# Inverting the delta-rule's triangular matrix: six doubling levels of 128 columns, or blocks of 4 by Horner steps, levels on 32 stacked columns and the last level applied to the right-hand sides

## The reference

```python
def rwkv7_scan(r, w, kk, kka, k, v, s0):
    def step(S, inp):
        r_t, w_t, kk_t, kka_t, k_t, v_t = inp
        sa = jnp.einsum('bzhvk,bzhk->bzhv', S, -kk_t)
        S = S * w_t[..., None, :] + sa[..., None] * kka_t[..., None, :] + v_t[..., None] * k_t[..., None, :]
        return S, jnp.einsum('bzhvk,bzhk->bzhv', S, r_t)
    ...
```

## Time and profile before

| | |
|---|---|
| median of 3 runs | 3470.89 us (3470.37 to 3471.7) |
| the profiled execution | 3465.07 us, its span 3463.3 us |
| mean granted clock of PE | 0.978 of full speed |
| busy, share of span | PE 95%, DVE 57%, ACT 31%, POOL 15% |
| HBM traffic | 93 GB/s |

### The profile page before, as it was taken

One profiled execution on the slowest core, in us unless ns is written; L12 is line 12 of the kernel. 1 busy time (PEld: TensorE's weight loads), 2 busy tenths in 40 slices (PEclk: granted clock), 3 DMA queues, 4 the chain that ended last, 5 costly groups with the idle time before them and its releaser, 6 DMA issues.

```text
span 3463.3 us, 52254 instructions
## 1 busy us (share of the span) xinstructions
PE 3283.2 (95%) x21464; PEld 3011.0 (87%) x21464; DVE 1978.7 (57%) x2613; ACT 1083.7 (31%) x1588; POOL 525.1 (15%) x537
## 2 busy tenths in 40 slices
PE   6999999999699989999999999999988999999998
PEld 6999878978598979998789998799767988899986
DVE  5677564565555766775657774625566566522235
ACT  2211352244322252112531113523442223511134
POOL 2000110003234430001100001100213434200010
PEclk8999999999799999999999999999988999999999
DMA  5334343210000043443434434421000002222135
GB/s 203 122 145 149 135 142 134 88 36 3 26 1 10 7 160 112 155 145 120 138 132 146 152 127 144 158 82 44 24 28 1 1 10 75 92 74 81 63 110 164
DMA packets 62899, 323.81 MB, mean 93 GB/s; under 512 B 8784, under 2 KB 12688, under 8 KB 43408
## 3 DMA queue, kind: packets, MB, share of 16 engines
q1 hardware_dynamic: 62736, 321.52, 26.4%
HBM read 318.18 MB, written 3.31 MB: 93 GB/s over the span
## 4 chain that ended last, share of the span: by engine, by line
PE 81%; DVE 10%; DMA 3%; ACT 3%; issue 2%; POOL 1%; SPq 0%; DVEq 0%; ACTq 0%; POOLq 0%
PE PS L2004 42%; PE PS L2087 14%; PE PS L1331 7%; DMA wo<-in_wo 3%; PE PS L2015 3%; PE PS L648 2%; PE PS L670 2%; DVE wo_lo L2391 1%; ACT wo_hi L2192 1%; DVE macc L1845 1%; PE PS L595 1%; PE PS L658 1%; PE PS L1324 1%; PE PS L1282 1%; DVE LK L1683 1%
## 5 line engine op out<-in xcount | busy, mean ns | idle before, releaser
L2004 PE MATMUL PS<-h_hi,wi_hi 128*128 128x384 f32 (+1 forms) x3360 | 799.9, 310 | 21.7 <-issue 13.5
L2004 PE MATMUL PS<-h_lo,wi_hi 128*128 128x384 f32 (+1 forms) x3360 | 797.7, 309 | 0.0
L2004 PE MATMUL PS<-h_hi,wi_lo 128*128 128x384 f32 (+1 forms) x3360 | 797.7, 309 | 0.0
L2004 PEld LDWEIGHTS PS<-h_hi,wi_hi 128*128 128x128 f32 x3360 | 526.7, 188 | 25.2 <-issue 16.1
L2004 PEld LDWEIGHTS PS<-h_lo,wi_hi 128*128 128x128 f32 x3360 | 526.7, 188 | 0.6
L2004 PEld LDWEIGHTS PS<-h_hi,wi_lo 128*128 128x128 f32 x3360 | 526.5, 188 | 0.6
L2087 PE MATMUL PS<-wo_hi,a_hi 128*128 128x512 f32 x968 | 393.3, 406 | 20.3 <-DVE wo_lo L2391 13.3
L2391 DVE TENSOR_TENSOR wo_lo<-wo,wo_hi 128x1024 fp32r<-128x1024 f32 x208 | 256.1, 1231 | 265.0 <-ACT wo_hi L2192 264.0
L2087 PE MATMUL PS<-wo_hi,a_lo 128*128 128x512 f32 x968 | 378.5, 391 | 0.0
L2087 PE MATMUL PS<-wo_lo,a_hi 128*128 128x512 f32 x968 | 378.4, 391 | 0.0
L1845 DVE SCALAR_TENSOR_TENSOR macc<-wm,csil,macc 128x512 f32<-128x512 f32 x476 | 366.3, 769 | 16.9
(11 more groups left out here) (302 smaller groups left out, 4627.4 us busy)
## 6 DMA issues: line engine op xcount, KB each, us to landing
wi<-in_wi SPq DMA_DIRECT2D x88, 1024.0 KB, 5.0
wo<-in_wo SPq DMA_DIRECT2D x176, 512.0 KB, 3.5
wm<-in_wm SPq DMA_DIRECT2D x36, 2048.0 KB, 7.9
wi<-in_win SPq DMA_DIRECT2D x24, 1024.0 KB, 5.0
wo<-in_wout SPq DMA_DIRECT2D x32, 512.0 KB, 3.5
x<-in_x SPq DMA_DIRECT2D x1, 2048.0 KB, 26.4
wq<-in_wq SPq DMA_DIRECT2D x2, 1024.0 KB, 4.7
out_y_sample<-x SPq DMA_DIRECT2D x4, 512.0 KB, 5.7
```

The costliest lines, as they stand in the source:

```text
L2004: mm = pe.matmul(PSF[0:cols, at:at + GW[g]], st, h[g][:, k, :], start=(k == 0 and q == 0), stop=(k == KD - 1 and q == 2))
```

## The change

The inverse is found another way, per chunk:

1. **Blocks of 4 by Horner.** `LM` is now LB masked to blocks of 4 (levels 0 and 1 together, written by DVE straight from PSUM, `fours`). Three rounds X = I + LM^T X give the inverse of these blocks, since the cube is the highest power that is not zero.
2. **Stacked operands.** As long as blocks are at most 32, the 32 columns of all four diagonal blocks are stacked: `Xc` is 128 x (4 heads x 32), the identity `stack32`. Its transpose, block-diagonal, is kept in `XT`: DVE transposes each 32x32 block in place (`diagonal`, four instructions per direction and level). Levels 2, 3 and 4: t1 = near^T Xc on PE, where `near` is one mask for these levels; DVE multiplies with the packed mask of the level into T1; dx = XT^T T1 on PE, added to Xc on DVE.
3. **Level 5** goes from 32 to 64: t1 and dx on 32 columns, T1 copied by ACT, the result transposed by DVE into the off-diagonal blocks of XT.
4. **The last level is applied and not formed:** XT (two 64-blocks) is applied to R; the near half of the result times the off-diagonal block of LB (64x64 tiles of PE, both directions side by side) gives Zs; the diagonal block applied to Zs is added to the far half of X by DVE.

LK's products go to banks 0 to 3 in place of 4 to 7. POOL writes two masks per direction and chunk in place of seven. The preps stand at other places between the levels. The phase's start gains three table reductions on DVE, two memsets of XT and four additions of masks on POOL. SP's weight load waits for the second tile set (`gh_mm`) in place of the last `dxt_mm`.

```diff
@@ rwkv_tensor, inner and solve @@
                     if which:
-                        until(pe, l, f"lb{d}", c + 1)
+                        for one in ("alpha_tok", "kappa_tok", "beta_tok", "v_tok", "bv"):
+                            until(pe, l, one, c + 1)
...
+                for k in range(3):
...
+                        group(4 + 2 * d, QUAD, lambda h: LM[d][:, h, :], lambda h: Xc[d][:, h, :] if k else stack32)\
+                            .then_inc(S[f"b_mm{d}"].sem, 1)
...
+                    lk_values(c)
+                    if c + 1 < NT:
+                        prep(c + 1, 0)
+                for lv in range(2, 6):
+                    for d in range(2):
+                        until(pe, l, f"lm{d}", 2 * c + (1 if lv < 5 else 2))
+                        until(pe, l, f"x{d}", 6 * c + lv + 1)
+                        group(4 + 2 * d, QUAD, lambda h: (near if lv < 5 else LM)[d][:, h, :],
+                              lambda h: Xc[d][:, h, :]).then_inc(S[f"t1_mm{d}"].sem, 1)
+                    for d in range(2):
+                        until(pe, l, f"lb{d}", c + 1)
+                        until(pe, l, f"t1{d}", 6 * c + lv - 1)
+                        until(pe, l, f"xt{d}", 5 * c + lv - 1)
+                        group(5 + 2 * d, QUAD, lambda h: XT[d][:, h, :], lambda h: T1[d][:, h, :])\
+                            .then_inc(S[f"dx_mm{d}"].sem, 1)
+                    if c + 1 < NT and lv in (3, 5):
+                        prep(c + 1, (3, 5).index(lv) + 1)
...
-                for lv in range(1, 7):
...
+                for d in range(2):
+                    until(pe, l, f"t1{d}", 6 * c + 5)
+                for h in range(NH):
+                    for d, (a, b) in enumerate(halves):
+                        mm = pe.matmul(PS[b, 4 + 2 * d, h * P:(h + 1) * P], LB[d][a, h, 0, b], X[d][a, h, :],
+                                       start=True, stop=True)
...
+                for d in range(2):
+                    until(pe, l, f"t1{d}", 6 * c + 6)
+                for h in range(NH):
+                    for d, (a, b) in enumerate(halves):
+                        mm = pe.matmul(PS[b, 5 + 2 * d, h * P:(h + 1) * P], XT[d][b, h, b], Zs[d][b, h, :],
+                                       start=True, stop=True)
...
@@ rwkv_vector @@
+            def diagonal(d, k):
+
+                for q in range(4):
+                    at = slice(q * QUAD, (q + 1) * QUAD)
+                    m = v_.transpose(XT[d][at, :, at], Xc[d][at, :, :])
+                m.then_inc(S[f"xt{d}"].sem, 1)
+
+            def level_out(c, d, lv):
...
+                v_.tensor_tensor(xc, xc, PS[:, 5 + 2 * d, 0:P], ALU.add).then_inc(S[f"x{d}"].sem, 1)
+                mm_(f"x{d}", 6 * c + lv + 2)
+                diagonal(d, lv)
...
+                for lv in range(2, 5):
+                    for d in range(2):
+                        mm_(f"t1_mm{d}", 5 * c + lv - 1)
+                        v_.tensor_tensor(T1[d][:], PS[:, 4 + 2 * d, 0:P].rearrange("p (h t) -> p h t", h=NH),
+                                         packed[:, d, lv - 2, :].unsqueeze(1).broadcast_to([P, NH, QUAD]), ALU.mult)\
+                            .then_inc(S[f"t1{d}"].sem, 1)
+                    for d in range(2):
+                        level_out(c, d, lv)
+                    if c + 1 < NT and lv in (2, 4):
+                        prep(c + 1, (2, 4).index(lv) + 1)
+                    if c == NL and lv > 2:
+                        beside(lv - 2)
...
+                if c + 1 < NT:
+                    prep(c + 1, 3)
                 if c == NL:
...
+                    beside(3)
+                    beside(4)
+                    beside(5)
+                for d in range(2):
+                    mm_(f"gh_mm{d}", c + 1)
+                    mm_(f"t1{d}", 6 * c + 6)
+                    b = slice(64, P) if d == 0 else slice(0, 64)
+                    half_ = X[d][b, :, :].rearrange("p h t -> p (h t)")
+                    v_.tensor_tensor(half_, half_, PS[b, 5 + 2 * d, :], ALU.add).then_inc(S[f"gh{d}"].sem, 1)
...
@@ rwkv_gpsimd, sync @@
             for c in range(NT):
-                for lv in range(7):
+                for lv in range(2):
...
-                        until(sp, l, f"dxt_mm{d}", 30)
+                        until(sp, l, f"gh_mm{d}", 5)
```

More of the change, by code:

```diff
@@ new lines, in solve @@
+                if c + 1 < NT:
+                    prep(c + 1, 2)
+                if c == NL:
+                    beside(3)
+                for d in range(2):
+                    until(a_, l, f"dx_mm{d}", 5 * c + 5)
+                    a_.activation(X[d][:].rearrange("p h t -> p (h t)"), PS[:, 5 + 2 * d, :], ACT.Copy)\
+                        .then_inc(S[f"t1{d}"].sem, 1)
+                if c == NL:
+                    beside(4)
+                for d in range(2):
+                    until(a_, l, f"t1_mm{d}", 5 * c + 5)
+                    b = slice(64, P) if d == 0 else slice(0, 64)
+                    a_.activation(Zs[d][b, :, :].rearrange("p h t -> p (h t)"), PS[b, 4 + 2 * d, :], ACT.Copy)\
+                        .then_inc(S[f"t1{d}"].sem, 1)
@@ L1593, in solve @@
+                if c == NL:
+                    beside(5)
+                    beside(6)
                 for d in range(2):
@@ L1717, in solve @@
+                if c < NL:
+                    for d in range(2):
+                        for q in range(2):
+                            a, b = (2 * q, 2 * q + 1) if d == 0 else (2 * q + 1, 2 * q)
+                            v_.memset(XT[d][a * QUAD:(a + 1) * QUAD, :, b * QUAD:(b + 1) * QUAD], 0.0)
+                if c == NL:
+                    beside(6)
                 for d in range(2):
@@ L1730, in solve, with beside @@
                     m.then_inc(S[f"n_out{d}"].sem, 1)
-            for part in range(4):
+            def beside(lv):
+                if lv >= 3:
+                    rwkv_gate(v_, l, lv - 3)
+                if 2 <= lv <= 5:
+                    gn_squares(v_, l, NT + lv - 2)
+                if lv <= NL:
+                    rwkv_centre(v_, l, lv - 1)
+            prep(0, 0)
+            mm_("four", 1)
+            for d in range(2):
+                v_.reduce_sum(packed[:, d, :, :], lvl[:, 1 - d, 2:5, :].rearrange("p l (j c) -> p l c j", c=QUAD), AX)
+            v_.reduce_sum(stack32, ident[:].rearrange("p (j c) -> p c j", c=QUAD), AX).then_inc(S["packed"].sem, 1)
+            for part in range(1, 4):
                 prep(0, part)
@@ L1807, in prep_kappa @@
                 po.tensor_tensor(kd[:], kd[:], Pinv[:], ALU.mult).then_inc(S["kappa"].sem, 1)
+            until(po, l, "rs_mm", 5)
+            for d in range(2):
+                po.memset(XT[d][:], 0.0)
+            po.tensor_tensor(lvl[:, :, 1, :], lvl[:, :, 1, :], lvl[:, :, 0, :], ALU.add).then_inc(S["four"].sem, 1)
             prep(0)
             prep_kappa(0)
+            until(po, l, "packed", 1)
+            for k, done in ((3, "near_a"), (2, "near_b"), (1, "near_c")):
+                po.tensor_tensor(lvl[:, :, 4, :], lvl[:, :, 4, :], lvl[:, :, k, :], ALU.add).then_inc(S[done].sem, 1)
+                until(po, l, done, 1)
             for c in range(NT):
-                for lv in range(7):
+                for lv in range(2):
                     for d in range(2):
```

228 lines of the change are left out of this document (136 added, 92 removed).

## The result

| | before | changed |
|---|---|---|
| median | 3470.6 us (3467.2 to 3471.7, 4 runs) | 3568.9 us (3566.2 to 3570.0, 4 runs) |
| ratio | | 1.0284, 95% interval 1.0266 to 1.0302 |
| span of the profiled execution | 3463.3 us | 3566.6 us |
| mean granted clock of PE | 0.978 | 0.921 |

What follows compares the result with a forecast made beforehand. PE was taken to bound the solver chunks. Eight middle chunks x 8.7 = 70, fifth chunks 8, prologues 3 and loads 2 make +83 on 3465.07, 3548; the median lies 5.8 higher: 3554 us, range 3425 to 3600.

Steps and rivals of the forecast that it cites:

- The clock decides the sign: Middle chunks: -7.2 us each if PE's clock stays at 1.00, +8.7 with the forecast's losses of clock to narrow operands.
- the two rows that the clock was argued from: Two-column matmuls at 10.8 to 38.1 us, 0.214 us each; one-column ones after 673.38, clock falling from 1.00 to 0.59.
- 32 columns save next to nothing in a group: PE groups of eight instructions: 32 columns cost 0.89 us like 128, and 1.71 us at the lower clock.
- The chunk at the upper clock: Middle chunk at granted 1.00: -31.2 - 5.2 + 19.7 + 1.8 + 7.7 = -7.2 us, a chunk of 49.6.
- rival C: DVE transposes take 0.33 us, each level's loop grows 0.6 us; with A 3434 us; chance 0.09, inside A's 0.18.
- The waits, 7.7 forecast: New PE waits in a middle chunk: Horner 0.4, levels 1.8, prep(2) 2.0, tail 3.5 us.
- What the clock costs a chunk: Stretches of a middle chunk at the lower clock add 15.9 us, making 65.5, 8.7 above 56.8.
- each dense prep restores it for a level: Levels of a middle chunk: preps bring the clock back, so levels 2 and 4 pay 1.2 us each, level 3 1.8.
- The fifth chunk: Chunk with the read-out on DVE: fin's adds stand behind three of its blocks, +4 us each, 8 (bounds 0 and +8 each).
- A: Rival: PE's clock stays at 1.00, 8 x -7.2 + 0 + 5 = -53, so 3418 us; chance 0.18, with C.
- B: Rival: prep and inner blocks restore the clock, a chunk costs about 57 us, 3481 give or take 25; chance 0.10.
- D: Rival: PE at the lower clock throughout, chunks of 71 us, +127, 3598 us; chance 0.12.

Runs made afterwards that it cites:

- moved128: Changed kernel with every 32-column matmul of Horner and levels 2 to 5 moving its columns four times, 128 in all; 3428.4 us, ratio 0.9889 to the kernel before.
- fifth128: Changed kernel with 128 columns moved in the fifth chunk only, 32 in the other four; 3533.8 us (one run).
- moved64: Changed kernel with the 32 columns of Horner and levels 2 to 5 moved twice, 64 in all; 3465.9 us (one run).
- before_moved32: Kernel before with level matmuls (t1, dx, dxt) moving only 32 of 128 columns, three quarters of the level products left out; 3754.1 us (one run).

## Why the prediction was right, and which terms were off

The forecast was 3554 us, slower because of the clock; it is 3569, inside the range. That it is only 15 us off is in part luck: the eight chunks were forecast 13.5 us too long and the fifth chunks 29.7 too short.

- **The clock decides the sign**: shown. With the columns moved four times, and nothing else changed but where the readers find them, the same program is 1.1% faster than the kernel before; narrowed, the kernel before is 8.3% slower.
- **One of the two rows that the clock was argued from is weaker than it was read.** For the earlier trace rows the spacing, 0.214 us an instruction, is that of the lower clock elsewhere, but the clock column of the same stretch says full speed:

```profile
12.00:38.00 26.00, 26.00 (x124) 1.00 0.89 379
```

The trace's clock record has its first entry at 41 us, so this 1.00 may stand for no record; which of the two is right stays open. And the 128-column products behind, at 0.218, are no faster, so this stretch does not tell that narrow operands were the reason. (0.59 behind one-column products, PE never idle) and the runs above carry the argument.
- **32 columns save next to nothing in a group**: 0.85 us at 1.00 against 0.89 for 128, and 1.71 at 0.50, as forecast.
- **The chunk at the upper clock** (two slips in its working, 0.56 for a wait that the rows have at 0.57 and 19.7 for 22 x 0.89 = 19.6, change nothing), forecast 49.6, is 50.2 in moved128 where it is at 1.00 throughout. The transposes' 0.26 was too low; it is 0.31, near the end that had been taken for rival C. The tile sets took 1.0 us (1056.28 to 1057.31 above) where I took 0.9. The waits, 7.7 forecast, are 6.7: Horner none (0.4), levels 1.7 (1.8), prep part 2 2.1 (2.0), the tail 0.78 + 1.35 + 0.75 (1.0 + 1.5 + 1.0).
- **What the clock costs a chunk**, by starts on PE, the chunk from 1054.41 against moved128's from 980.21:

| stretch | forecast | measured |
|---|---|---|
| Horner | +1.1 | +0.4 (5.7 to 6.1) |
| LK's group | +1.75 | +1.8 (1.8 to 3.6) |
| prep part 0 | +1.6 | +1.4 (1.6 to 3.0) |
| levels 2, 3, prep part 1 | +4.75 | +6.4 (10.8 to 17.2) |
| levels 4, 5 | +2.2 | +3.6 (9.9 to 13.5) |
| prep part 2 | +1.9 | +1.2 (1.9 to 3.1) |
| R, tiles, fin | +2.6 | 0 (14.7 both) |
| sum | +15.9 | +14.7 (50.2 to 64.9) |

The sum is near by errors that cancel. The step "each dense prep restores it for a level" was the wrong one: prep parts 0 and 1 run at 0.50 themselves (but for the end of part 1), and part 0 restores nothing. Behind part 1 the clock is back in six of the eight chunks (1025.87 above), but for 3.4 us only, half of level 4. The table's chunk is one of the two where it isn't. The other, too high a charge for what follows level 5, failed the other way: the clock comes back during the transposes of part 2 (0.21 us apart at first, 0.11 at the end), before the R groups, so in layer 1 everything from there runs as in moved128. The four chunks of layer 2 gain 3.4 us at 1.00 in level 4 and have 3.4 us at 0.50 in the tail, where the table's chunk has none; the second of them has its windows here:

```profile
2773.20:2776.50 3.30, 3.30 (x31) 3.30 (x32) 1.65 (x6) 0.62 (x2) 1.26 (x1) 1.00 0.00 0
2793.60:2797.00 3.40, 3.40 (x33) 3.28 (x33) 1.25 (x6) 0.00 (x0) 0.00 (x0) 0.50 0.00 0
```

The eight chunks came to +56.5 and not +70: against the forecast's 65.5 each layer's first (63.2) is 2.3 us shorter, one (61.6) 3.9, the other five 0.6 to 0.7, and the first chunks of before were 0.6 and 0.9 longer than the 56.8 that I took for all.
- **The fifth chunk** is the term that was wrong: "+4 each, 8 (bounds 0 and +8 each)", measured +21.2 and +16.5, outside its bounds. I gave it VectorE's part only and charged the clock to the eight middle chunks alone, though its levels are the same 32-column groups and its read-out products move 64 columns. fifth128 gives back 30.6 of the 37.7 us; in moved128 all but 1.6 are gone, so VectorE's part, put at 8, was too high as well. What its blocks take alone was not measured.
- **Rivals.** A (clock stays, 3418) and C with it (3434) are what moved128 measures by other means, 3428. B (near no change, 3481 give or take 25) is close to what moved64 does with twice the columns, 3466. D (low throughout, chunks of 71) did not happen: most of the tail of the chunk is at 1.00. That the hand-offs alone bind, which is no rival of the prediction but theory 2 here, fell with moved128.
- By the Trainium skill ("TensorE: Matmul & The Clock Gate", "Why this matters for your kernels") matmul bursts want no long idle gaps between them. No run here contradicts that, but it was not enough: at 998 to 1003 the clock falls, and from 1009.00 to 1022.60 it stays at 0.50, with PE busy throughout.

Why the clock came back behind prep part 1 in six chunks and not in the other two, and why it fell again in the tail of layer 2's, was not tried.

## What to carry to other kernels

Count instructions before columns: here an instruction with 128 weight columns took 0.11 us at granted 1.00 whether it moved 32 columns or 128, and a long stretch of narrow ones took PE to half its clock, so read the granted clock of every stretch whose operands shrink. If an algorithm's operands become narrow, move them several times side by side into unused PSUM and measure; here four times the columns cost 0.04 us a group (0.89 against 0.85). Charge such a loss to every chunk that holds the narrow work, the odd one with other work beside it first of all.

## What the runs showed of the hardware that was not expected

- Less work was slower by 287 us, more than the 100 to 220 expected: the kernel before with a quarter of the columns in its level products (3754 us against 3467).
- The loss has a middle: in the chunk shown 64 columns held 1.00 through Horner and level 2 and lost it in level 3, at a wait that 128 columns passed at 1.00; with 96 columns the run is within 4 us of 128.
- Matmuls of 256 columns between narrow ones did not bring the clock back at once: eight of prep part 1 run at the lower clock in the changed kernel from 1022.67 and in before_moved32 from 1055.57, 0.40 to 0.44 us apart. At their end it was back for 3.4 us in six of the changed kernel's eight chunks and in two of before_moved32's.
- The clock can go at a wait too: in moved128's chunk of 52.2 us PE waits 2.46 us ahead of prep part 2 (the clock is 1.00 from 1061 to 1064 and 0.50 from 1065 to 1067) and then issues its transposes 0.21 us apart, at half the rate; in the chunk of 50.2 us, after 2.11 us, they are at 0.11.
